# Scores of a latent attention, from fp32 products to three fp32r products of high parts and rests

## The reference, cut to what matters

```python
# shared keys and values, from a latent of 512
kv = rmsnorm(h @ w_kv_a[:, :512]) @ w_kv_b      # per head: k_nope (128), v (128)
k_rope = rope(h @ w_kv_a[:, 512:])              # 64, one for all heads
# queries, from a latent of 768
q = rmsnorm(hn @ w_q_a) @ w_q_b                 # per head: q_nope (128), q_rope (64)
scores = (q_nope . k_nope + q_rope . k_rope) * 192 ** -0.5
out = softmax(mask(scores)) @ v                 # then @ w_o
```

## Time and profile before

| | |
|---|---|
| median of three runs | 1326.72 us |
| profiled execution | 1326.18 us |
| its span | 1324.4 us |
| TensorE matmul busy | 1291.5 us (98%), 9416 instructions |
| VectorE busy | 816.1 us (62%), 1477 instructions |
| ScalarE busy | 607.7 us (46%), 1031 instructions |
| mean granted TensorE clock | 0.992 |

### The profile page before, as it was taken

How to read it: one execution, slowest core, us unless ns; L and a number is a source line. 1 busy time by engine, 2 the same in 40 slices (tenths; PEclk the granted TensorE clock), 3 DMA queues, 4 the chain that set the end, 5 groups by cost and what they waited for, 6 DMA issues and landing times. The chain is left out here.

```text
span 1324.4 us, 24380 instructions
## 1 busy us (share of the span) xinstructions
PE 1291.5 (98%) x9416; PEld 1124.2 (85%) x9416; DVE 816.1 (62%) x1477; ACT 607.7 (46%) x1031; POOL 55.0 (4%) x97
## 2 busy tenths in 40 slices
PE   6999999999999999999999999999999999999996
PEld 5999999999999998789999998988999974444444
DVE  6477567588776677567888766867655852222224
ACT  4555545444444464555444446666644541111112
POOL 0100011000000000000000000000000000000000
PEclk8999999999999999999999999999999999999999
DMA  9775456566667653225667776442144759999994
GB/s 378 166 239 186 143 162 204 186 214 221 213 221 239 210 168 128 96 91 193 234 230 237 240 241 235 163 128 80 49 159 164 246 200 401 399 424 426 426 425 166
DMA packets 71189, 295.76 MB, mean 223 GB/s; under 512 B 9718, under 2 KB 10742, under 8 KB 60208
## 3 DMA queue, kind: packets, MB, share of 16 engines
q1 hardware_dynamic: 58896, 257.38, 53.8%
q0 software_dynamic: 12192, 36.95, 9.3%
HBM read 287.76 MB, written 11.53 MB: 226 GB/s over the span
## 5 line engine op out<-in xcount | busy, mean ns | idle before, releaser
L2163 DVE TENSOR_TENSOR ring_low<-ring,w_hi 128x1024 fp32r<-128x1024 f32 x292 | 355.2, 1223 | 184.4 <-ACT w_hi L1683 183.1
L862 PE MATMUL bank<-hn_hi,w_hi 128*128 128x272 f32 (+1 forms) x1416 | 411.7, 291 | 4.4 <-DVE hn_low L2184 3.9
L866 PE MATMUL bank<-hn_hi,ring_low 128*128 128x272 f32 (+1 forms) x1416 | 405.4, 286 | 0.0
L865 PE MATMUL bank<-hn_low,w_hi 128*128 128x272 f32 (+1 forms) x1416 | 404.5, 286 | 0.0
L1683 ACT ACTIVATE w_hi<-ring 128x1024 fp32r<-128x1024 f32 x292 | 302.4, 1051 | 124.8 <-PE bank L862 111.7
L862 PEld LDWEIGHTS bank<-hn_hi,w_hi 128*128 128x128 f32 x1416 | 268.5, 190 | 8.1 <-DVE hn_low L2184 4.4
L866 PEld LDWEIGHTS bank<-hn_hi,ring_low 128*128 128x128 f32 x1416 | 268.7, 190 | 0.0
L865 PEld LDWEIGHTS bank<-hn_low,w_hi 128*128 128x128 f32 x1416 | 268.4, 190 | 0.3
L862 PE MATMUL bank<-arena_r,w_hi 128*128 128x256 f32 (+1 forms) x784 | 224.6, 287 | 2.3 <-DVE arena L2411 2.2
L866 PE MATMUL bank<-arena_r,ring_low 128*128 128x256 f32 (+1 forms) x784 | 223.1, 285 | 0.0
L865 PE MATMUL bank<-arena_r,w_hi 128*128 128x256 f32 (+1 forms) x784 | 222.7, 284 | 0.0
(11 more groups left out here) (469 smaller groups left out, 1653.6 us busy)
## 6 DMA issues: line engine op xcount, KB each, us to landing
ring<-weights SPq DMA_DIRECT2D x300, 512.0 KB, 3.5
ring<-pairs_in SPq DMA_DIRECT2D x42, 1024.0 KB, 13.4
mod_part<-mod_rows POOLq DMA_DIRECT2D x40, 512.0 KB, 4.7
w_late<-pairs_in SPq DMA_DIRECT2D x14, 1024.0 KB
tab<-pairs_in SPq DMA_DIRECT2D x14, 1024.0 KB
arena<-pairs_in SPq DMA_DIRECT2D x12, 1024.0 KB, 14.9
ring<-pairs_in SPq DMA_DIRECT2D x12, 512.0 KB, 4.4
tab<-tables SPq DMA_DIRECT2D x1, 2858.0 KB, 17.5
```

The costliest lines, as they stand in the source:

```text
L862: begun = mm(dst[:, 0:cols], wh, high(k), start=k == 0, stop=False)
L865: mm(dst[:, 0:cols], wh, low(k), start=False, stop=False)
L866: last = mm(dst[:, 0:cols], wl, high(k), start=False, stop=k == K - 1)
L2163: tt_(ring_lo[:, slot, :], ring[:, slot, :], w_hi[:, n % SPLITS, :], ALU.subtract).then_inc(S("w_lo_ready"), 1)
```

## The change

The scores' operands are split like those of the dense products. The high parts of keys and queries are the ScalarE copies that stored them before, now rounded to fp32r (`k_m_hi`, `q_m_hi`), and the rests are made by VectorE from the same PSUM banks (`head_low`), which frees the banks from now on. ScalarE's copies count up one semaphore, `head_high`, whose value at each of them is listed in the dictionary of that name. The rope parts are split too: five copies on ScalarE (`rope_high`) and five subtractions on VectorE (`rope_low`), once. Each score block then consists of six fp32r matmuls in place of two fp32 ones. The rests of three heads at a time lie in a part of `hn_hi` (`HEAD_LOWS`). In VectorE's program `kq_low(0)` to `kq_low(2)` and the five `rope_low` come before the loop over heads, and `kq_low(i + 3)` takes the place of `lows(at["qn", i + 3])` at the end of its body. Elsewhere some semaphores are merged (`exp_rows` and `dec_exp` into `decay_exps`, `beta_ready` and `softplus_ln` into `beta_softplus`), with the same waits in the same places; that part of the diff is left out here.

```diff
          + D * (3 * 512 + 3 * 512 + 512 + 2 * D) + 2 * 512 * D + D * D + NE * 3 * D * EF) // (P * UNIT)
 
 ARENA = 18560
+HEAD_LOWS = 3
...
-        q_m = carve(MH, SEQ, at=0)
+        q_m_hi = carve_r(MH, SEQ, at=0)
...
-        krope = carve(1, T0, at=cq_at + 2 * QT * SEQ)
-        k_m = carve(MH, T0)
+        krope_at = cq_at + 2 * QT * SEQ
+        krope, krope_lo = place(krope_at, 1, T0)
+        k_m_hi = carve_r(MH, T0, at=krope_at + T0)
         v_m = carve(3, MH * P)
-        qrope = carve(4, SEQ)
-        mrope_t = carve(2, T0)
+        qrope_at = cursor[0]
+        qrope, qrope_lo = place(qrope_at, 4, SEQ)
+        mrope_t = carve(2, T0, at=qrope_at + 4 * SEQ)
+        krope_hi = carve_r(1, T0)
+        hn_hi_flat = hn_hi[:, :, :].rearrange("p a b -> p (a b)")
+        low_at = HEAD_LOWS * T0, HEAD_LOWS * (T0 + SEQ)
+        k_m_lo = hn_hi_flat[:, 0:low_at[0]].rearrange("p (a b) -> p a b", a=HEAD_LOWS)
+        q_m_lo = hn_hi_flat[:, low_at[0]:low_at[1]].rearrange("p (a b) -> p a b", a=HEAD_LOWS)
+        qrope_hi = [hn_hi_flat[:, low_at[1] + n * SEQ:low_at[1] + (n + 1) * SEQ] for n in range(2)]
+        qrope_hi += [carve_r(1, SEQ)[:, 0, :] for _ in range(2)]
...
+        head_high = {}
+        for name in ([("krope", 0), ("kn", 0), ("qn", 0), ("kn", 1)] + [("qrope", t) for t in range(4)]
+                     + [("qn", 1), ("kn", 2), ("qn", 2)]):
+            head_high[name] = len(head_high) + 1
+        for j in range(MH + 2):
+            for name, n in (("am", j - 2), ("kn", j + 3), ("qn", j + 3)):
+                if 0 <= n < MH:
+                    head_high.setdefault((name, n), len(head_high) + 1)
...
             def mla_score(i, dst):
-                if i == 0:
-                    pe.wait_ge(S("q_roped"), 5)
+                if i % 2 == 0:
+                    pe.wait_ge(S("rope_split"), 2 + i // 2)
                 wait_stored(pe, at["kn", i])
                 wait_stored(pe, at["qn", i])
                 if i >= 2:
@@ -1167,8 +1186,13 @@
                 r = 64 * (i % 2)
                 for lo, hi, q0 in [(0, META + P, 0), (META + P, MLA_W, P)]:
                     w = hi - lo
-                    mm(dst[:, lo:hi], q_m[:, i, q0:q0 + P], k_m[:, i, 0:w], start=True, stop=False)
-                    last = mm(dst[:, lo:hi], qrope[r:r + ROPE, i // 2, q0:q0 + P], krope[r:r + ROPE, 0, 0:w],
+                    rows, slot = slice(r, r + ROPE), i % HEAD_LOWS
+                    mm(dst[:, lo:hi], q_m_hi[:, i, q0:q0 + P], k_m_hi[:, i, 0:w], start=True, stop=False)
+                    mm(dst[:, lo:hi], q_m_hi[:, i, q0:q0 + P], k_m_lo[:, slot, 0:w], start=False, stop=False)
+                    mm(dst[:, lo:hi], q_m_lo[:, slot, q0:q0 + P], k_m_hi[:, i, 0:w], start=False, stop=False)
+                    mm(dst[:, lo:hi], qrope_hi[i // 2][rows, q0:q0 + P], krope_hi[rows, 0, 0:w], start=False, stop=False)
+                    mm(dst[:, lo:hi], qrope_hi[i // 2][rows, q0:q0 + P], krope_lo[rows, 0, 0:w], start=False, stop=False)
+                    last = mm(dst[:, lo:hi], qrope_lo[rows, i // 2, q0:q0 + P], krope_hi[rows, 0, 0:w],
                               start=False, stop=True)
...
             def k_tile(t):
                 tile[0] = at["kn", t]
-                src, free = take()
-                fn(k_m[:, t, :], src[:, 0:T0], ACT.Copy).then_inc(free, 1)
+                src, _ = take()
+                fn(k_m_hi[:, t, :], src[:, 0:T0], ACT.Copy).then_inc(S("head_high"), 1)
+
+            def rope_high(n, hi, x):
+                act.wait_ge(S("q_roped"), n)
+                fn(hi, x, ACT.Copy).then_inc(S("head_high"), 1)
...
             def q_nope(t):
                 tile[0] = at["qn", t]
-                src, free = take()
-                fn(q_m[:, t, :], src[:, 0:SEQ], ACT.Copy).then_inc(free, 1)
+                src, _ = take()
+                fn(q_m_hi[:, t, :], src[:, 0:SEQ], ACT.Copy).then_inc(S("head_high"), 1)
...
             v_turned(0)
+            rope_high(1, krope_hi[:, 0, :], krope[:, 0, :])
             v_turned(1)
-            for t in range(3):
-                k_tile(t)
-                q_nope(t)
+            k_tile(0)
+            q_nope(0)
+            k_tile(1)
+            for t in range(4):
+                rope_high(t + 2, qrope_hi[t], qrope[:, t, :])
+            q_nope(1)
+            k_tile(2)
+            q_nope(2)
...
             def mla_store(j):
                 tile[0] = am(j)
                 src, _ = take()
-                fn(o_m_hi[:, j, :], src[:, 0:SEQ], ACT.Copy).then_inc(S("om_hi_ready"), 1)
+                fn(o_m_hi[:, j, :], src[:, 0:SEQ], ACT.Copy).then_inc(S("head_high"), 1)
...
             for t in range(4):
                 rotate_tile(qr_tile(t), qrope[:, t, :], META, SEQ)
-            for t in range(3):
-                lows(at["kn", t])
-                lows(at["qn", t])
+
+            def rope_low(name, lo, x, hi):
+                dve.wait_ge(S("head_high"), head_high[name])
+                tt_(lo, x, hi, ALU.subtract).then_inc(S("rope_split"), 1)
+
+            def head_low(name, i, lo, hi, cols):
+                src, free = take(at[name, i])
+                dve.wait_ge(S("head_high"), head_high[name, i])
+                tt_(lo, src[:, 0:cols], hi, ALU.subtract).then_inc(free, 1)
+
+            def kq_low(i):
+                head_low("kn", i, k_m_lo[:, i % HEAD_LOWS, :], k_m_hi[:, i, :], T0)
+                head_low("qn", i, q_m_lo[:, i % HEAD_LOWS, :], q_m_hi[:, i, :], SEQ)
+
+            kq_low(0)
+            rope_low(("krope", 0), krope_lo[:, 0, :], krope[:, 0, :], krope_hi[:, 0, :])
+            for t in range(4):
+                rope_low(("qrope", t), qrope_lo[:, t, :], qrope[:, t, :], qrope_hi[t])
+            kq_low(1)
+            kq_low(2)
...
-                dve.wait_ge(S("om_hi_ready"), j + 1)
+                dve.wait_ge(S("head_high"), head_high["am", j])
...
                 if 3 <= i:
                     o_m_low(i - 3)
                 if i + 3 < MH:
-                    lows(at["qn", i + 3])
+                    kq_low(i + 3)
...
```

More of the change, by code:

```diff
@@ L1288, in _ @@
             pe.wait_ge(S("dec_diff"), 1)
-            pe.wait_ge(S("exp_rows"), 1)
+            pe.wait_ge(S("decay_exps"), 1)
             pe.wait_ge(S("l2_inverted"), 1)
@@ L1943, in _ @@
             act.wait_ge(S("ba_split"), 2)
-            fn(M("beta", 0, 8), M("b", 0, 8), ACT.Sigmoid).then_inc(S("beta_ready"), 1)
+            fn(M("beta", 0, 8), M("b", 0, 8), ACT.Sigmoid).then_inc(S("beta_softplus"), 1)
             fn(M("sp", 0, 8), M("abs", 0, 8), ACT.Exp, scale=-1.0)
@@ L1947, in _ @@
             act.wait_ge(act_step, 1)
-            fn(M("sp", 0, 8), M("sp", 0, 8), ACT.Ln, bias=eps_t[:, 2:3]).then_inc(S("softplus_ln"), 1)
+            fn(M("sp", 0, 8), M("sp", 0, 8), ACT.Ln, bias=eps_t[:, 2:3]).then_inc(S("beta_softplus"), 1)
             def conv_silu(first):
@@ L1968, in _ @@
                 last = fn(TM[:, 4 * j:4 * j + 4, :], bank[6 + j][:, :].rearrange("p (a b) -> p a b", a=4), ACT.Exp)
-            last.then_inc(S("exp_rows"), 1)
+            last.then_inc(S("decay_exps"), 1)
             highs(at["qka"])
             act.wait_ge(S("dec_diff"), 1)
-            fn(decT[:, :, :], decT[:, :, :], ACT.Exp).then_inc(S("dec_exp"), 1)
+            fn(decT[:, :, :], decT[:, :, :], ACT.Exp).then_inc(S("decay_exps"), 1)
             tile[0] = at["qka"]
@@ L2517, in _ @@
             stt(M("abs", 0, 8), M("a", 0, 8), -1.0, M("a", 0, 8), ALU.mult, ALU.max).then_inc(S("ba_split"), 1)
-            dve.wait_ge(S("beta_ready"), 1)
-            dve.wait_ge(S("softplus_ln"), 1)
+            dve.wait_ge(S("beta_softplus"), 2)
             link(stt(M("sp", 0, 8), M("a", 0, 8), 0.0, M("sp", 0, 8), ALU.max, ALU.add))
@@ L2549, in _ @@
             lows(at["qka"])
-            dve.wait_ge(S("exp_rows"), 1)
+            dve.wait_ge(S("decay_exps"), 1)
             for p in range(NP):
@@ L2555, in _ @@
             last.then_inc(S("dec_diff"), 1)
-            dve.wait_ge(S("dec_exp"), 1)
+            dve.wait_ge(S("decay_exps"), 2)
             link(tt_(decT[:, :, :], decT[:, :, :], spread(C("upto"), NP), ALU.mult))
```

## The result

The changed kernel takes 1348.68 us (median of 6 runs, 1337.28 to 1355.46), the kernel before beside it 1326.26 (1324.86 to 1327.0): ratio 1.0158, 95% interval 1.0134 to 1.0183. I had forecast 1332.3, in a range of 1328 to 1338: slower, as said, but by four times as much. The ratios here are taken over the fast runs, which leaves out one slow run in the whole document (1352.78 us of "before + longer wait"), and they are not quotients of the medians, from which they lie about 0.1% off, and 0.5% for that kernel. The profiled execution of after took 1347.7 us, span 1345.5.

A forecast was written before the change was run, and what follows sets the result against it. TensorE, busy nearly throughout, was taken as the bound. Opening to head 1's turn +3.25, three periods +3.65, end -0.61 and -0.67 sum to +5.6 us: 1332.3 from 1326.72, 8-in-10 range 1328 to 1338.

The forecast's parts named there:

- The wait: Before the turns of heads 1 to 4: serial chain of 1.96 us where 0.12 were, TensorE losing 1.84 us each.
- the work itself: Subtraction of `kn`, weight rests beside the head's products, and ScalarE's copies were to cost nothing.
- The score: Twelve fp32r products per head take 1.42 us (1.16 to 1.56), 0.67 less than 2.09.
- a change between fp32 and fp32r: At the head's first 12 products: such a change costs about 0.1 us.
- The three periods: Turns of heads 2, 3 and 4: 9.11 us each instead of 7.88, +3.65 us in all.
- the two terms of the end: After the turn of head 4: -0.61 us up to the next turn, -0.67 from the last score.
- rival 3: Clock falls in the new idle times, up to 1.7 us per fall; two falls 1335.7, six 1342; 20%.
- The opening: Before the loop: score 0 waits for VectorE's rests, starting at 526.85 (+2.00 us); +3.25 in all by head 1's turn.
- rival 1: Faster: the scores' gain arrives in full, 5.7 us, giving 1321.0; 10%.
- rival 2: Only the waits per head are paid, the opening's stall being caught up: -2.4 on the sum, 1329.9; 10%.
- rival 4: A 144-column product runs at fp32's four rows per column: score 2.4 us, no gain, time 1340; 3%.

The follow-up runs named there:

- before + longer wait: Kernel before, VectorE also waiting at loop end for ScalarE's stores of head i + 3, then making one extra subtraction; 1343.29 us, ratio 1.0082.
- mended, 4 changes: Changed kernel with only ScalarE's and VectorE's order altered (rope and head 0 rests earlier, loop making rests of i + 2), product order kept; 1324.58 us, ratio 0.9995.
- one depth: Changed kernel's twelve products and ScalarE copies without rests, rope products taking all 128 rows; 1321.19 us, ratio 0.9966.
- the stacked score: Changed kernel with ScalarE and VectorE reordered, and three 64-row rope products made as two of 128 rows; 1316.14 us, ratio 0.9928.
- All stops filled: Changed kernel, waits kept, with unread products in TensorE's stops before score 0 and the turns of heads 0 to 4; 1336.61 us, ratio 1.0078.
- rests one head later: Changed kernel with rests of head i + 2, not i + 3, made at the end of VectorE's loop body; 1327.16 us, ratio 1.0020.
- opening mended: Changed kernel with rope parts split earlier and head 0's rests ahead of the weight rests, loop unchanged; 1347.84 us, ratio 1.0173.
- before + wait alone: Kernel before, with VectorE also waiting at loop end until ScalarE has stored both tiles of head i + 3; 1329.26 us, ratio 1.0039.
- five stops filled: Changed kernel, waits kept, with 14 unread products in each stop before score 0 and the turns of heads 1 to 4; 1343.38 us, ratio 1.0124.

## Why the prediction was wrong

**The wait: right.** Last product 562.05, copy 562.37, subtraction 562.86, reciprocal 563.20, turn 564.01: 1.96 us, the chain that I had counted, with each of its links. Turns 1, 2 and 3 of after lie 9.71 and 9.69 apart (554.30, 564.01, 573.70) where I had 9.11; the difference is the score. Turns 5 and 6 don't wait, as said. That the work itself costs nothing holds too, to within 0.2% (mended, 4 changes).

**The score: the mis-sized term.** "A score is then 1.42 us (1.16 to 1.56)" failed; it is 2.09 (and 1.50 with one depth). Both durations in it, 0.11 and 0.127, were right. What I left out is that two of the four groups have 64 rows: each change of depth costs 0.17 us, four of them 0.67 us, and this is the whole gain. The rows of before gave only the pairs `x2` at the scores' lines, so I priced all twelve products by 128-row rows, without a bound for a change of depth.

The term stood in the earlier trace rows all the same, under another name. I put the 0.1 us at the head's first products down to "a change between fp32 and fp32r". In the timeline of before, what stands ahead of them is a product of 16 rows:

```profile
563.22 0.69 PE L1205 MATMUL bank<-hn,arena 16*128 16x256 f32 x2
...
564.07 0.29 PE L865 MATMUL bank<-arena_r,w_hi 128*128 128x272 f32 x1
```

From the head's first product (563.84) to the second it is 0.23 us, 0.10 more than between equal neighbours, and after has the same 0.23 where a 272-column product follows 64 rows. Behind the 128-row fp32 transposes of a turn, where the kind changes and the depth doesn't, the first product of the score takes 0.15 for 0.11 (564.53 to 564.68), and behind the stacked score, where neither changes, the head's first takes 0.12 (535.75 to 535.87). So most of that 0.1 belonged to the depth, and two such changes, into the rope part and out of it, stand in each block of a score.

The missing 0.67 us can't be multiplied by eight, because turns 0 and 1 wait for VectorE and hide a part. By my own paths turn 0 then stands 0.57 later, at 539.8, and turn 1 is behind it by turn, score, head and wait: 0.55 + 2.09 + 3.77 + 1.84 = 8.25 us, at 548.05, +4.12 for +3.25. The three periods become 9.78 us each, +5.66 for +3.65, and the two terms of the end +0.06 and 0 for -0.61 and -0.67. The sum is 9.8 us for 5.6, and the time 1336.6. All stops filled has turn 0 at 539.67, turn 1 at 547.89 and turn 5 9.3 us late, and costs 11.0 in the medians. After's fastest run, 1337.28, had a mean clock of 0.994, no lower than that of before's profiled execution (0.992).

The Trainium skill's isolated spacing by columns ("TensorE: Matmul & The Clock Gate", section "Back-to-back issue gap"), by which 144 columns would take 62.5 ns, is too low here: the row shows 0.11 us. The section says itself that this formula under-counts where each product also loads its own weights, and gives about 81 ns for 128 columns there, which the row is above, too. The Trainium skill's load time for 128 columns on the same page (section "LDWEIGHTS (loading the stationary operand)"), 107 ns, agrees with the row.

**The clock: the mis-weighed rival.** "What TensorE does before and behind the stops here is dense, as at 509, so 20%" failed. I held one stop that kept the clock against one that lost it and took the first for the rule. In after's trace the clock fell behind three of the stops: from 527.2 to 534.1 behind score 0's (1.94 us of idle time), from 544.3 to 551.1 behind turn 0's, from 575.0 to 585.3 behind turn 3's. It did not fall behind those of turns 1, 2 and 4, which show the same 1.68 us of idle time as that of turn 3; turn 0's is the shortest, 1.41:

```profile
543.14 0.33 PE L1203 MATMUL bank<-tab,hn 128*128 128x128 f32 x1 [1.41 <-DVE hn L2517]
...
573.70 0.33 PE L1203 MATMUL bank<-tab,hn 128*128 128x128 f32 x1 [1.68 <-DVE hn L2517]
...
587.87 0.33 PE L1203 MATMUL bank<-tab,hn 128*128 128x128 f32 x1 [1.68 <-DVE hn L2517]
```

By the clock sum the three falls cost 3.4 + 3.4 + 5.1 us; rival 3's price of up to 1.7 for a fall held for its 3.3 us at the lower level, but here a fall lasted two or three times that. With 1336.6 this gives 1348.5; the profiled execution took 1347.7, the median is 1348.68. Shown: the falls come from the turns' stops (rests one head later ends them, opening mended doesn't), with fp32 scores as well (before + longer wait), and go when TensorE has anything to do (all stops filled).

**The opening** was roughly right. Score 0 started at 527.15 for 526.85, after 1.94 us of idle time. Turn 1 came 10.37 us late; less 6.8 of clock 3.6, where the sum with a score of 2.09 us has 4.1 and all stops filled shows 3.96. At the end, turns 4 to 5 took 4.10 us, not 3.50: again the score.

Rivals 1, 2 and 4 found no support. Adding up the turns, 20.2 of the span's 21.1 us stand at turn 7 (578.12 to 598.30). The other 0.9 isn't the change's: it arises among the last 500 matmuls, which take 96.1 us in before's profiled execution, 97.0 in after's and 96.6 to 97.4 in those of the twelve other kernels, before + wait alone (96.8) among them.

**Open:** why 1.54 us more in front of a turn hardly ever ends in a fall and 1.84 so often does, and why equal stops of one execution differ. The length alone doesn't decide: the twelve stops with 1.68 us of idle time in the profiled executions of after, before + longer wait and after, opening mended were followed by three falls, the four of 1.33 us of before + wait alone by none, and yet the stop of turn 0, with only 1.41 us, goes with a fall in all three executions that have it (after; five stops filled; opening mended). No run varied what TensorE does around a stop of fixed length.

## What to carry to other kernels

A split of a fresh tile must not stand in an in-order engine's list ahead of the work that the bound engine waits for next: one turn later was worth some 20 us here, with the same instructions. Price a product by its depth and its neighbours' too, not by its columns alone; stack two 64-row products into one of 128 where an operand can be laid out for it. And where a change makes a dense TensorE stop for some 2 us again and again, count the lower clock as likely, not as a tail.

## What the runs showed of the hardware

A change between 128- and 64-row fp32r products costs 0.17 us (periods of 7.81, 7.46 and 7.13 us with 4, 2 and 0 changes), half of it ahead of the first product of the new depth and half behind. Stops with 1.4 to 1.9 us of idle time in dense work were followed by the lower clock level for 3.4 to 10.2 us in some cases and not at all in others of the same execution, which spreads a kernel's runs over 18 us; unread products in the stops narrowed this to 1.2.
